# Norms of a two-layer trunk, taken block by block instead of tensor by tensor

## The reference, cut to what matters

```python
def rmsnorm(x, g):
    x32 = x.astype(f32)
    y = x32 * lax.rsqrt(jnp.mean(x32 * x32, axis=-1, keepdims=True) + EPS) * g.astype(f32)
    return y.astype(x.dtype)
...
        h = rmsnorm(x, norm_g[l, 0]) * (1 + sc1) + sh1
        ...                                   # y = mixer(h), ends in a projection y @ w_out
        x = x + (1 + g1) * rmsnorm(y, norm_g[l, 1])
        h = rmsnorm(x, norm_g[l, 2]) * (1 + sc2) + sh2
        y = swiglu(h, ffn_w_gate[l], ffn_w_up[l], ffn_w_down[l])
        x = x + (1 + g2) * rmsnorm(y, norm_g[l, 3])
```

## Time and profile before

| | |
|---|---|
| median of 3 runs | 2991.62 us (2991.14 to 2992.17) |
| the profiled execution, its own time | 2992.33 us |
| its span in the trace | 2990.6 us |
| TensorE busy | 2687.0 us, 90% |
| VectorE, ScalarE, GpSimd busy | 1261.9, 1071.0, 967.4 us |
| mean granted clock of TensorE | 0.947 |

### The profile page before, as it was taken

One profiled execution on the slowest core, in us unless ns is written; L12 is line 12 of the kernel. 1 busy time (PEld: TensorE's weight loads), 2 busy tenths in 40 slices (PEclk: granted clock), 3 DMA queues, 4 the chain that ended last, 5 costly groups with the idle time before them and its releaser, 6 DMA issues.

```text
span 2990.6 us, 35461 instructions
## 1 busy us (share of the span) xinstructions
PE 2687.0 (90%) x12576; PEld 2193.1 (73%) x12576; DVE 1261.9 (42%) x1451; ACT 1071.0 (36%) x1610; POOL 967.4 (32%) x402
## 2 busy tenths in 40 slices
PE   4999999989899999999999997666889999999995
PEld 2777778767678887788877786554667888788884
DVE  5566644333720155201567413766473005430145
ACT  2444443343433333333332223544343333322222
POOL 0111110004344444344434443211334444344442
PEclk7999999999899999999999998888999999999998
DMA  6233332043223332232346543111222333233232
GB/s 235 64 99 105 107 92 78 29 167 101 71 84 98 97 93 91 84 98 92 98 134 225 185 160 106 43 56 42 71 71 87 96 98 98 84 98 97 92 99 91
DMA packets 91097, 300.38 MB, mean 100 GB/s; under 512 B 9793, under 2 KB 10113, under 8 KB 91009
## 3 DMA queue, kind: packets, MB, share of 16 engines
q1 hardware_dynamic: 91008, 299.20, 31.4%
HBM read 275.05 MB, written 24.12 MB: 100 GB/s over the span
## 4 chain that ended last, share of the span: by engine, by line
issue 57%; PE 27%; POOL 11%; DVE 2%; DVEq 1%; ACT 1%; POOLq 1%; ACTq 0%
POOL w_lo L462 10%; PE ps L503 6%; PE ps L504 6%; PE ps L507 6%; PE ps L774 3%; PE ps L780 3%; PE ps L777 3%; POOL ybuf L473 1%; POOL arena L473 1%; DVEq L1222 0%; POOLq L476 0%; DVEq L1494 0%; DVE h_lo L1194 0%; ACT w_hi L828 0%; DVE ybuf L1186 0%
## 5 line engine op out<-in xcount | busy, mean ns | idle before, releaser
L462 POOL TENSOR_TENSOR w_lo<-w_raw,w_hi 128x1024 fp32r<-128x1024 f32 x370 | 909.4, 2461 | 1797.6 <-ACT w_hi L828 1293.5
L503 PE MATMUL ps<-h_hi,w_hi 128*128 128x512 f32 x2448 | 991.0, 405 | 85.8 <-ACT w_hi L828 54.7
L504 PE MATMUL ps<-h_lo,w_hi 128*128 128x512 f32 x2448 | 977.5, 399 | 0.0
L503 PEld LDWEIGHTS ps<-h_hi,w_hi 128*128 128x128 f32 x2448 | 474.6, 194 | 216.8 <-issue 78.3
L507 PE MATMUL ps<-h_hi,w_lo 128*128 128x512 f32 x2448 | 606.9, 390 | 0.0
L828 ACT ACTIVATE w_hi<-w_raw 128x1024 fp32r<-128x1024 f32 x346 | 363.9, 1057 | 632.0 <-PE ps L507 320.8
L504 PEld LDWEIGHTS ps<-h_lo,w_hi 128*128 128x128 f32 x2448 | 475.7, 194 | 97.0 <-issue 0.5
L507 PEld LDWEIGHTS ps<-h_hi,w_lo 128*128 128x128 f32 x2448 | 461.5, 189 | 96.4
L1598 DVE TENSOR_TENSOR arena<-arena,ps 128x512 f32 (+1 forms) x88 | 60.5, 688 | 782.6 <-PE ps L507 782.6
L1613 DVE TENSOR_TENSOR a_lo<-arena,a_hi 128x512 fp32r<-128x512 f32 x88 | 211.6, 2404 | 212.8 <-ACT a_hi L1149 212.5
L774 PE MATMUL ps<-a_hi,w_hi 128*128 128x512 f32 x704 | 174.3, 390 | 6.6 <-ACT a_hi L1149 6.6
(11 more groups left out here) (174 smaller groups left out, 2267.8 us busy)
## 6 DMA issues: line engine op xcount, KB each, us to landing
w_raw<-weights SPq DMA_DIRECT2D x370, 512.0 KB, 3.5
arena<-ada_w SPq DMA_DIRECT2D x80, 512.0 KB, 3.6
proj<-arena SPq DMA_DIRECT2D x24, 512.0 KB, 3.4
x<-xT SPq DMA_DIRECT2D x4, 2048.0 KB, 11.1
arena<-ada_w SPq DMA_DIRECT2D x4, 2048.0 KB, 20.2
arena<-proj SPq DMA_DIRECT2D x8, 1024.0 KB, 4.8
arena<-proj SPq DMA_DIRECT2D x8, 512.0 KB, 4.1
y_hi_d<-a_hi SPq DMA_DIRECT2D x7, 512.0 KB, 2.6
```

What stands on the lines that cost most here:

```text
L462: pool.tensor_tensor(w_lo[:, s, :], w_raw[:, s, :], w_hi[:, s, :].bitcast(f32), ALU.subtract).then_inc(lo_done, 1)
L503: pe.matmul(bank(b), w, high[:, k, :], start=k == 0, stop=False)
L504: pe.matmul(bank(b), w, low[:, k, :], start=False, stop=False)
```

## The change

Squares, sums and updates are cut up into blocks.

- The tensor `sq` is gone. Each square of a pre-norm or of a down projection's output is a 128x512 Square that ScalarE writes to PSUM bank 6 or 7 in turn (`squares`); VectorE adds it to `acc_b` (`sums`), and the square after the next waits for that. `squares` of a pre-norm stand at positions 2 (blocks 0 to 3) and 3 (4 to 7), `sums` likewise.
- In the out projections ScalarE reads every bank twice, with a Square and with a Copy, and rounds the unit after the next first (`hi_next`); VectorE evicts nothing; GpSimd adds the squares, between its `w_lo` (`out_norms`). The mean of the post-norm stands behind unit 0 of half 1, that of the pre-norm behind unit 4.
- `scaled` is gone. `update` works by pairs of blocks: two SCALAR_TENSOR_TENSORs write y times gain times reciprocal to banks 4 and 5, and one TENSOR_TENSOR of 128x1024 adds them to x. Pairs 0 and 1 stand at position 1, pairs 2 and 3 at position 2.
- In layer 0, h of the FFN is written during units 5 to 7 of the out projection's half 1.
- The last row of `down` runs bank by bank (`last_row`), and each bank is read as it is done. Its first row starts with banks 4 to 7, and only bank 0 waits for the products of gate/up; `a_hi` waits for its own block alone.
- After the last down, each bank is squared as it is done, the products are taken from PSUM, and GpSimd adds six blocks to x, VectorE two.

```diff
-        sq = arena[:, 11776:15872].rearrange("p (k t) -> p k t", k=KB)
+        norm_buf = arena[:, 11776:14848].rearrange("p (k t) -> p k t", k=6)
+        acc_y, acc_b, sq_tile = [norm_buf[:, 0, :], norm_buf[:, 1, :]], norm_buf[:, 2, :], [norm_buf[:, 3 + i, :] for i in range(3)]
...
+            def out_norms(layer):
+
+                for half in range(2):
+                    done = 2 * layer + half
+                    for m in range(KB):
+                        use = USE_OUT[layer] + KB * half + m + 2
+                        lo(use, use % 2)
+                        if m:
+                            pool.wait_ge(ysq_done, 8 * done + m + 1)
+                            pool.tensor_tensor(acc_y[half], acc_y[half], sq_tile[m % 2], ALU.add).then_inc(ysq_read, 1)
+                            pool.drain()
+                    pool.drain().then_inc(yacc_done, 1)
...
+            for i, k in enumerate(LAST_POOL):
+                pool.wait_ge(t_last, i + 1)
+                xs = x[:, k, HALF:S]
+                pool.tensor_tensor(xs, xs, y3[:, k, :], ALU.add).then_inc(x_fin_p, 1)
...
-                            if post and (i, s) == (0, 1):
+                            if post and (i, s) == (0, 0):
                                 mean(*post[0])
-                            if pre and (i, s) == (PAIRS_OUT - 1, 0):
+                            if pre and (i, s) == (2, 0):
...
+                    for m in order:
+                        if first and m == 0:
+                            pe.wait_ge(free0, tiles + 1)
+                            pe.wait_ge(free1, tiles + 1)
...
+                def last_row():
+
+                    u, slot = use + FB - 1, (use + 1) % 2
+                    pe.wait_ge(hi_done, u + 1)
+                    pe.wait_ge(ah_done, FB * (d + 1))
+                    pe.wait_ge(al_done, FB * (d + 1))
+                    pe.wait_ge(lo_done, u + 3)
+                    for j, m in enumerate(LAST_BANKS if d == 3 else range(KB)):
+                        pe.matmul(bank(m), w_hi[:, slot, cols[m]], a_hi[:, 1, :], start=False, stop=False)
+                        pe.matmul(bank(m), w_hi[:, slot, cols[m]], a_lo[:, 1, :], start=False, stop=False)
+                        pe.matmul(bank(m), w_lo[:, slot, cols[m]], a_hi[:, 1, :], start=False, stop=True)\
+                            .then_inc(dn_done if j < KB - 1 else unit_used, 1)
...
+            def squares(layer, kind, half, first=0, last=KB):
+
+                site = square_site(layer, kind, half)
+                if kind == 3:
+                    a.wait_ge(dn_ev1, 4 * (dn_idx(layer, half) + 1))
+                    a.drain()
+                for k in range(first, last):
+                    if kind != 3 and k % 2 == 0:
+                        a.wait_ge(x_part, 4 * upd(layer - (kind == 0), 3 if kind == 0 else 1, half) - 3 + k // 2)
+                    if 8 * site + k > 1:
+                        a.wait_ge(sq_read, 8 * site + k - 1)
+                    src = y3[:, k, :] if kind == 3 else x[:, k, half * HALF:(half + 1) * HALF]
+                    a.activation(bank(6 + k % 2), src, ACT.Square).then_inc(sq_done, 1)
...
+            def hi_next(use):
+                a.wait_ge(raw_full[use % 2], 16 * (use // 2) + 16)
+                a.activation(w_hi[:, use % 2, :], w_raw[:, use % 2, :], ACT.Copy).then_inc(hi_done, 1)
...
                     at.setdefault(n, []).append((f, args))
+                if post and post[0][1] == 3:
+                    put(-1, squares, *post[0])
                 if post:
-                    put(-1, square, *post[0], post[1])
-                    put(0 if phase == "out" else 1, root, *post[0])
+                    put(1, root, *post[0])
                 if pre:
-
-                    put(1.5 if phase == "out" else 3, square, *pre, None)
-                    put(2.5 if phase == "out" else 5, root, *pre)
+                    put(2, squares, *pre, 0, 4)
+                    put(3, squares, *pre, 4, 8)
+                    put(5, root, *pre)
...
+                    for m in range(KB):
+                        a.wait_ge(unit_used, base + m + 3)
+                        hi_next(base + m + 2)
+                        if 0 < m < 3:
+                            if job:
+                                a.wait_ge(ysq_read, 7 * job)
+                        elif m:
+                            a.wait_ge(ysq_read, 7 * job + m - 2)
+                        a.activation(sq_tile[m % 2] if m else acc_y[half], bank(m % 4), ACT.Square).then_inc(ysq_done, 1)
+                        a.activation((y3, y_out1)[half][:, m, :], bank(m % 4), ACT.Copy).then_inc((free0, free1)[m % 2], 1)
+                        if half and m in (0, 4):
+                            root(layer, 1 + m // 4, 0)
+                        if half and m in (2, 3):
+                            squares(layer, 2, 0, 4 * m - 8, 4 * m - 4)
+                        if half and m > 4 and layer == 0:
+                            for k in ((0,), (1, 2, 3), (4, 5, 6, 7))[m - 5]:
+                                write_h(k, None, USE_OUT[0] + KB, (0, 2, 0))
+                if layer:
+                    for k in range(KB):
+                        write_h(k, None, ffn_base(layer, 0), (layer, 2, 0))
...
-                        if u == 0:
-                            a.wait_ge(free1, tiles + FB + 1)
+                        a.wait_ge(free1, tiles + u + 2)
                         a.activation(a_hi[:, u % 2, :], act[:, u, :], ACT.Copy).then_inc(ah_done, 1)
...
+                    if (layer, half) == (1, 1):
+                        for j, m in enumerate(LAST_BANKS):
+                            if j < KB - 1:
+                                a.wait_ge(dn_done, 7 * d + j + 1)
+                            else:
+                                a.wait_ge(unit_used, base + FB + 2)
+                            a.activation(act[:, m, :], bank(m), ACT.Square).then_inc(sq_done, 1)
+                            if j == 0:
+                                a.activation(y3[:, m, :], bank(m), ACT.Copy).then_inc(dn_ev0, 1)
+                        root(1, 3, 1)
+                        continue
+                    a.wait_ge(hl_done, 8 * (h_job(nl, nk, nh) + 1))
                     for m in range(0, KB, 2):
+                        a.wait_ge(dn_done, 7 * d + m + 1)
                         a.activation(y3[:, m, :], bank(m), ACT.Copy).then_inc(dn_ev0, 1)
-                        if m in (2, 4) and (layer, half) != (1, 1):
-                            hi_at(base + FB, 0, m // 2 - 1)
-            square(1, 3, 1, y3)
-            root(1, 3, 1)
+                        if m == 4:
+                            hi_at(base + FB, 0, 0)
+                    hi_at(base + FB, 0, 1)
...
+            def sums(layer, kind, half, first=0, last=KB):
+
+                site = square_site(layer, kind, half)
+                for k in range(first, last):
+                    v.wait_ge(sq_done, 8 * site + k + 1)
+                    if k == 0:
+                        v.tensor_copy(acc_b, bank(6)).then_inc(sq_read, 1)
+                    else:
+                        v.tensor_tensor(acc_b, bank(6 + k % 2), acc_b, ALU.add).then_inc(sq_read, 1)
+                    if k < KB - 1:
+                        v.drain()
+                    else:
+                        v.drain().then_inc(bsum_done, 1)
...
+            def update(layer, kind, half, y, first=0, last=4):
 
                 g = 8 * (4 * layer + kind)
-                v.drain()
-                if (layer, kind) == (0, 1):
-                    v.wait_ge(x_again, 32)
-                for k in range(KB):
-                    xs = x[:, k, half * HALF:(half + 1) * HALF]
-                    op = v.scalar_tensor_tensor(xs, y[:, k, :], gain[:, g + k:g + k + 1], xs, ALU.mult, ALU.add)
-                    if (layer, kind, half) == (1, 3, 1):
-                        op.then_inc(x_final, 1)
-                v.drain().then_inc(x_upd, 1)
+                if kind == 1 and first == 0:
+                    v.wait_ge(free0, T_OUT[layer] + PAIRS_OUT * (half + 1) + 1)
+                    v.wait_ge(free1, T_OUT[layer] + PAIRS_OUT * (half + 1) + 1)
+                if (layer, kind, first) == (0, 1, 0):
+                    v.wait_ge(x_again, 16 + 16 * half)
+                for i in range(first, last):
+                    for s in range(2):
+                        v.scalar_tensor_tensor(bank(4 + s), y[:, 2 * i + s, :], gain[:, g + 2 * i + s:g + 2 * i + s + 1],
+                                               rinv[:, 2, :], ALU.mult, ALU.mult)
+                    v.drain()
+                    xs = x[:, 2 * i:2 * i + 2, half * HALF:(half + 1) * HALF]
+                    v.tensor_tensor(xs, xs, ps[:, 2048:3072].rearrange("p (k t) -> p k t", k=2), ALU.add).then_inc(x_part, 1)
+                    v.drain()
...
-                    put(-1, sum_squares, *post[0])
-                    put(0 if out else 1, inverse, *post[0])
-                    put(0 if out else 1, scaled, post[1])
```

(71 more changed lines are left out.)

144 lines of the change are left out of this document (53 added, 91 removed).

## The result

The kernel after takes 3022.22 us (median of 4 runs, 3021.32 to 3023.32) against 2991.89 for the kernel before beside it (4 runs, 2991.14 to 2992.84): a ratio of 1.0101, 95% interval 1.0084 to 1.0119. The profiled execution took 3022.53 us with a span of 3020.7, 30.1 us more than before. TensorE's mean granted clock went from 0.947 to 0.940.

A forecast was written before the change was run, and what follows sets the result against it. TensorE, busy 90% of the span, was taken as the bound, so only its waits and clock matter. Terms 44.1+11.8+0.5-13.1-6.8-13.2 = +23.3 on 2992.33 gave 3015.6, less 0.7 for the median: 3015 us, range 2998 to 3028.

The forecast's parts named there:

- the give-back: Input projection, layer 1, half 0: block sums ending earlier shorten the root's stop, returning 2.3 us and 2.4 of clock.
- Term (a), the gate/up sites: Three gate/up phases hosting both norms: squares at positions 2 and 3 delay weight rounding; 14.7 us each, +44.1 together.
- Term (a), the input projection: Layer 1, half 0: the same stops plus two adaLN accumulations, 16.4 us, less what earlier block sums return; net +11.8.
- Terms (b) and (c), down: Down projections: bank-by-bank reading removes stops behind three, -13.1 us; earlier start removes stops ahead of four, -6.8.
- Term (d), the out stages: Out projections: pre-norm's mean waits 8.9 us against earlier stops removed; layer 0 -4, layer 1 +4.5, together +0.5.
- The light lock: Rival for the out stages: pre-norm's mean waits 3.3 us, not 8.9, in both layers; 3004 us, chance 0.13.
- Term (e), the tail: Behind the last matmul: 19.8 us to the end of the span instead of 33, so -13.2.
- The pieces really are sooner: Rival: ScalarE isn't held at positions 2 and 3 in the four host phases; about 2955 us, chance 0.10.
- GpSimd as too slow: Rival: GpSimd's add costs 2 us, each out-stage pair loses 1.5 and the tail 4; about 3027 us, chance 0.09.

The follow-up runs named there:

- Sums first: Kernel after with VectorE's sums of squares 0 and 1 moved ahead of the second half of the update: 2999.9 us, ratio 1.0023.
- squares later: Kernel after with ScalarE's pre-norm squares at positions 3 and 4 instead of 2 and 3: 2972.04 us, ratio 0.9924.
- down alone: Kernel before with only the bank-by-bank down projection, its start at banks 4 to 7 included: 2977.41 us, ratio 0.9951.
- squares spread: Kernel after with squares at positions 3.5 and 4.5, sums at 3 and 4, host-phase roots behind the next pair's roundings: 2931.40 us, ratio 0.9802.
- all three: Kernel after with squares spread, host-phase roots behind the next pair's roundings, and out-stage pre-norm mean behind unit 5: 2918.39 us, ratio 0.9758.

## Why the prediction was right

The forecast of 3015 was 7 us under the measured time, and the mechanism was the one it named. Two terms had a wrong part in them, the give-back in the input projection and the wait in layer 1's out stage; in the second, two errors partly cancelled.

- *Term (a), the gate/up sites: right, 1.8 us small in all.* Forecast 9.5 us before unit 6, measured 9.55, 9.56 and 9.55; 4.0 before unit 8, measured 4.01, 3.93 and 3.93. ScalarE waited between squares 1 and 2, for the copy that the working named. The pair cost 2.80. What was small is the clock in layer 0, half 0: the windows above have 18 and 20 matmuls in 7 us where 31 fit at 0.227 us, so 2.9 and 2.5 us were lost, 5.4 together; 3.7 was forecast. Sums first and squares later show the cause by experiment.
- *Term (a), the input projection: the mechanism right, the give-back wrong.* 11.8 forecast, 14.3 measured. I let the earlier sums shorten the root's stop from 4.07 to 1.81. It became 3.42, because ScalarE still sat 10.48 us for a store (10.97 before). The two things that the change brings to this phase work against each other, which the working left out: down alone, with the sums as before, made the stop 6.17, so the sooner start of the phase cost 2.1 us at the root and the rest of the change took 2.75 off. Nor did the two accumulations, for which the working added 1.7 us, lengthen the stop before unit 6: it was 9.48.
- *Terms (b) and (c), down: right.* -19.9 forecast (with the last down's start), measured -17.5 over three stretches and -1.6 at the last down's start, -19.1 together. For the part by itself the stretches have 18.3, 1.8 of it tail, and the ratio 14.7; both would be more without the idling that came back in the input projection.
- *Term (d), the out stages: the sum right, its parts not quite.* +0.5 forecast, -2.7 and +3.2 measured. That the sum agrees is partly luck. In layer 0 the mean waited 8.85 where 8.9 was forecast. In layer 1 it waited 5.15: there the first pair began ahead of `w_lo`, and the four pairs' products took 1.42, 3.19, 1.89 and 2.50 us, 9.0 in all, against 12.0 in layer 0. So the working had this wait 3.7 us too large, but the stage came out only 1.3 us shorter than forecast: of the 3.2 us by which that stretch grew, 3.0 are 128x512 matmuls that stand further apart than before, a term of clock that the working put at nothing for this stage. How the 783.4 of layer 0 was reached the working doesn't show; the unit was done at about 784.9. The rule cited from the Trainium skill (page SBUF — State Buffer, section Who interferes with whom) held for the case that no row had shown: with an output in PSUM two SBUF inputs still block, 4.54 us against 1.42 for two products; the add with one SBUF input took 1.220 to 1.222 us in all 28 cases, six of them beside work of GpSimd. The light lock, the rival that rested on the opposite, didn't come, though layer 1's 5.15 lies nearer to its 3.3 than to 8.9.
- *Term (e), the tail: right, 1.7 small.* -13.2 forecast, -11.5 measured. The last reciprocal starts 4.5 us behind the last matmul's start, where the working had 3.8; and from VectorE's last add (it ends at 3016.41) to the end of the span it is 4.3 us instead of 3.4.
- *The rivals.* "The pieces really are sooner" was wrong for this order of the queues, and right for another: with the squares where VectorE is free the sites are shorter than before. GpSimd as too slow falls: its add lasts 1.30 us, 1.74 where it takes turns with VectorE, and without it in half 1 the median was 3.6 us lower, which is within the intervals. Its price was also added up wrongly: eight pairs at 1.5 and 4 in the tail are 16 us, so 3031 and not 3027, above the 3028 that the range ends with.

The +6.8 between forecast and profile are +4.2 at the sites, +0.8 at the downs, +0.1 in the outs and +1.7 in the tail. Open stays the last stop of the input projection (5.70 us with the squares spread, 4.96 with all three; the longest stop there before was 4.07). It follows a store through a single buffer and VectorE's late copy ahead of it; that a second buffer would remove it is not shown, since no kernel with one was run.

## What to carry to other kernels

Work cut into pieces and shared by two engines through two buffers moves at the pace of the slower queue: ask for each piece what stands ahead of its partner in the other engine's program order, and what is queued behind the one that waits. Here one line of order was worth 22 us and the right positions of squares, sums, roots and a mean 104, with the same arithmetic. Compute for each position the time between the work's release and the next deadline (here the rounding, one unit of 5.44 us), and put waits that nobody needs soon, such as a root, behind the work with the deadline. Take each host phase by itself; the one with a store in its loop behaved unlike the three others.

## What the runs showed of the hardware

- A SCALAR_TENSOR_TENSOR of VectorE with two SBUF inputs and its output in PSUM stands against GpSimd's SBUF work: 746 ns at least, 2884 at most, the longest beside `w_lo` alone. The update's TENSOR_TENSOR with one input in SBUF and one in PSUM never did: 1220 to 1222 ns, also in the six cases beside GpSimd.
- A stop costs more than its idling. Behind 9.55 us of idling TensorE made 18 matmuls in 7 us at a granted 0.56, partly at 1.2 GHz, against the 31 that start in 7 us at 0.227 us apart. Taking out 5.2 us of idling in layer 1's out stage gave 7.8 us.
- Not every stop costs clock. Over the same 56 us of gate/up, layer 0, half 0, the granted clock was 1.00 with all three changes, where TensorE never idled, and 1.00 in the kernel before, which has stops of 1.81 and 2.40 us in it; in the kernel after, with 9.55 and 4.01 us, it was 0.82. Behind 2.32 us elsewhere in the kernel before it was 0.76. The kernel after and the kernel before:

```profile
786.00:842.00 56.00, 40.63 (x153) 31.84 (x152) 23.36 (x24) 15.24 (x20) 16.54 (x7) 0.82 0.18 56
...
786.00:842.00 56.00, 51.79 (x226) 41.95 (x225) 29.11 (x17) 18.23 (x18) 23.31 (x10) 1.00 0.30 87
```
